# A transformer trunk on one core: gate and up by Strassen's scheme, with the first sum of weight blocks on GpSimd

## The chip, the core and the metric

The kernel runs on one core of a Trainium2 chip. The metric is the device time of one execution in microseconds (us). The kernel before takes 2266.12 us (median of 3 runs, 2264.7 to 2266.59).

## What is computed

The input is 512 rows of 1024 channels, and 16 learned rows are put in front of them, which makes 528 tokens. Four layers follow. Each is a mixer (pooling, differential attention, a conformer convolution, pooling again) and a SwiGLU feed-forward block, both added to the residual stream `h`; at the end there is an RMS norm. The change touches the feed-forward block alone:

```python
def swiglu_ffn(h, w_gate, w_up, w_down):
    return (jax.nn.silu(h @ w_gate) * (h @ w_up)) @ w_down
...
h = h + swiglu_ffn(rmsnorm(h, norm_ffn_g[i]), ffn_w_gate[i], ffn_w_up[i], ffn_w_down[i])
```

`w_gate` and `w_up` are 1024 x 2816 and `w_down` is 2816 x 1024, all float32. The last layer needs only the 512 real tokens.

## The kernel before

**Precision.** Every product of two float32 matrices is made of three products in the faster `fp32r` type. Each operand is split into a high part (a copy in `fp32r`, made by ScalarE) and a low part (the operand minus its high part, made by VectorE). TensorE then adds up hi x hi, hi x lo and lo x hi; `chunk` (L639) issues these three for one 128 x 128 block of weights. All data lies transposed: channels on the 128 partitions, tokens along the free axis. In layers 0 to 2 the 528 tokens are taken as two halves of 264, so a block of weights costs 6 matmuls of 264 columns. In layer 3 it costs 3 matmuls of 512 columns.

**The feed-forward block.** The 2816 hidden channels are 22 blocks of 128, called f. For each f, `pair_layer` (L714) makes gate and up: for either matrix 8 blocks of weights, one below the other, are summed in PSUM (the accumulator memory, 8 banks of 512 columns). That is 96 matmuls of 264 columns for one f, or 48 of 512. Banks 0 to 3 and 4 to 7 take turns. `out_layer` (L778) makes the down projection: for each of the 8 output blocks d, 22 blocks of weights, which is 132 matmuls.

**The weights.** A tile of weights (1024 columns, 512 KB) is loaded by SyncE's DMA queue into one of 4 slots of `w_raw`, copied to `w_hi` by ScalarE (`split_hi`, L1138), and subtracted into `w_lo` by VectorE (`split_lo`, L1354). TensorE waits for `lo_ready`, and a slot of `w_hi` is free again at `tile_used`.

**Order on the engines.** Each engine has its own program, written out by hand, and they meet by semaphores. `rounds` (L1152 for ScalarE, L1410 for VectorE) sets the order: the splits of the tiles two ahead, and then the epilogue of a block. The epilogue of an f (`pair`, L1527) is: VectorE scales gate and up out of PSUM by `rstd` (L1532, L1534), ScalarE takes the silu (L1192), VectorE multiplies (`hid`, L1538), ScalarE makes `hid_hi` (L1194) and VectorE `hid_lo` (L1540). The epilogue of a d adds the PSUM result to `h` (L1511) and makes the next layer's input `y_hi` (L1143) and `y_lo` (L1360). GpSimd squares the blocks of `h` and adds them up for the next norm (`sum_squares`, L532: L545 and L548). In the feed-forward block it does nothing else.

**Drain.** Where a VectorE instruction reads what the one before it wrote, the program puts a `drain` between them, as in the convolution (L1783).

Of the kernel before, what the change touches and what calls it, by code (L numbers as in the profile page):

```python
# [26 lines left out]
F32 = mybir.dt.float32  # L27
F32R = mybir.dt.float32r
I32 = mybir.dt.int32
ALU = mybir.AluOpType  # L30
# [24 lines left out]
LAM_INIT = 0.8 - 0.6 * math.exp(-0.3 * 1)  # L55
SLOT = 1024
SLOTS = 4
DOWN_SPLIT = (6, 6, 5, 5)
SPILL = 512 - HALF - META
MASKED = -1e30  # L60
LOWEST = -3e38
# [47 lines left out]
def plan():  # L109

    cols, first = [], {}

    def phase(name, sizes):
        first[name] = len(cols)
        cols.extend(sizes)
        assert len(cols) % SLOTS == 0

    for layer in range(4):
        if layer in (0, 3):
            phase(f"pool{layer}", [512] * 4)  # L120
# [6 lines left out]
        phase(f"up{layer}", [1024] * (2 * NF))  # L127
        phase(f"down{layer}", [n * P for n in DOWN_SPLIT] * NB)
    return cols, first


class Placer:
# [12 lines left out]
class Memory:  # L145


    def __init__(self, nc, ctx):
# [46 lines left out]
        self.pooled = new("pooled", [P, 2, TOK])  # L195

        new = Placer(nc, keep, end)
        self.hid_hi = new("hid_hi", [P, NF * TOK], F32R)
        self.hid_lo = new("hid_lo", [P, NF * TOK], F32R)
# [3 lines left out]
        self.hid = new("hid", [P, TOK])  # L203

        new = Placer(nc, keep, end)
        self.bias = new("bias", [P, HEADS * TOK])
# [61 lines left out]
class Semaphores:  # L268


    def __init__(self, sem):
# [72 lines left out]
        self.cv_lo_ready = sem("cv_lo_ready")  # L344
        self.out_turned = sem("out_turned")
        self.out_ready = sem("out_ready")


def wait(eng, sem, value):

    if not (isinstance(value, int) and value <= 0):
        eng.wait_ge(sem, value)
# [45 lines left out]
def trunk(nc, a, out):  # L398
# [3 lines left out]
    with ctx:  # L402
# [10 lines left out]
        def blk(t, d, t0=0, n=TOK):  # L413

            return t[:, ds(d * TOK + t0, n)]
# [5 lines left out]
        def banks(b, half):  # L421

            return ps[:, b, 0:SEQ] if half == SEQ else ps[:, b:b + 2, 0:half]

        block = ctx.enter_context(nc.Block())


        @block.sync
        def _(sp):
# [50 lines left out]
                             0, n * P)  # L480

            def load_ffn(layer):
                load_pairs(f"up{layer}", a["ffn_w_gate"][layer], a["ffn_w_up"][layer], NF)
                load_out(f"down{layer}", a["ffn_w_down"][layer], DOWN_SPLIT, 2)

            load_pool("pool0", 0)

# [30 lines left out]
        def _(pool):  # L518
# [13 lines left out]
            def sum_squares(r, hn):  # L532


                wait(pool, s.token_sums, r)
                wait(pool, s.rstd_sums, r)
                pool.memset(m.sumsq[:, :], 0.0)
# [32 lines left out]
            pool.drain().then_inc(s.rel_ready, 1)  # L570
            sum_windows(0)
            sum_squares(R_FFN0, H_POOL0)
            sum_squares(R_ATTN, H_FFN0)

            pool.wait_ge(s.tile_used, first["attn"])
# [37 lines left out]
                row_factors(hd - 1)  # L613
            row_factors(HEADS - 1)
            sum_squares(R_FFN1, H_ATTN)
            sum_squares(R_CONV, H_FFN1)
# [7 lines left out]
            sum_squares(R_FFN2, H_CONV)  # L624
            sum_squares(R_POOL3, H_FFN2)

            pool.wait_ge(s.tile_used, first["pool3"])
# [3 lines left out]
            pool.drain()  # L631
            sum_windows(1)
            sum_squares(R_FFN3, H_POOL3)
            sum_squares(R_FINAL, H_FFN3)


        @block.tensor
        def _(pe):
# [189 lines left out]
                        part(g, k)  # L828

            def ffn(layer, r, yn, hn, t0=0, half=HALF):  # L830
                e0 = NF * layer + (NB if layer >= 2 else 0)
                pair_layer(f"up{layer}", NF, e0, r, yn, hn, t0, half)
                out_layer(f"down{layer}", hn + 1, m.hid_hi, m.hid_lo, DOWN_SPLIT, 2, s.hidden_ready, NF * layer,
                          [(s.pairs_read, e0 + NF - 1), (s.pairs_read, e0 + NF)], t0, half)

            def project(h, par, c, k0, k1):

# [232 lines left out]
            attention_end()  # L1070
            ffn(1, R_FFN1, Y_FFN1, H_ATTN)

            pair_layer("conv_in", NB, 2 * NF, R_CONV, Y_CONV, H_FFN1, 0, HALF, conv=True)
            def fill(n):

                for _ in range(n):
# [52 lines left out]
        def _(act):  # L1129
            def split_hi(t, i, per, n):  # L1130

                if n == 0:
                    return
                slot = t % SLOTS
                act.wait_ge(raw_in[slot], (i * (per // SLOTS) + (t // SLOTS + 1)) * 16)
                if t >= SLOTS:
                    act.wait_ge(s.tile_used, i * per + (t - SLOTS + 1))
                act.activation(m.w_hi[:, slot, 0:n], m.w_raw[:, slot, 0:n], ACT.Copy).then_inc(s.hi_ready, 1)  # L1138
# [46 lines left out]
                        split_hi(tile0 + 4 + g, 0, 0, cols[tile0 + 4 + g])  # L1185

            def ffn(layer, hn, yn, row, t0=0, n=TOK):
                f0 = NF * layer

                def pair(f):  # L1190
                    act.wait_ge(s.gate_ready, f + (f0 + 1))
# [4 lines left out]
                rounds(f"up{layer}", NF, 2, NF // 2, pair)  # L1196
                rounds(f"down{layer}", NB, 4, NB // 2,
                       lambda d: None if row is None else y_hi(d, hn, yn, row, 0, TOK))

            def exponentials(h, j):  # L1200
# [103 lines left out]
            def conv_gate(c):  # L1304
                par = conv_parity[0] % 2
                conv_parity[0] += 1
                wait(act, s.conv_done, c - 1)
                for tap in range(TENSOR_TAPS):
                    for dst, w in ((m.tap_hi, m.vec_hi), (m.tap_lo, m.vec_lo)):
                        e = act.activation(dst[:, par, tap, :], m.ident[:, :], ACT.Copy,  # L1310
                                           scale=w[:, ds(c * ROWS + (ROW_DW + tap), 1)].bitcast(F32))
                e.then_inc(s.taps_ready, 1)
                act.wait_ge(s.pairs_read, c + (2 * NF + 1))
# [33 lines left out]
        def _(dve):  # L1347
# [173 lines left out]
                rounds(name, NB, per_group, n_rounds, low, None, early, add)  # L1521

            def ffn(layer, r, yn, row, t0=0, half=HALF):
                f0, e0, n = NF * layer, NF * layer + (NB if layer >= 2 else 0), SEQ if half == SEQ else 2 * half
                parity = [0]

                def pair(f):  # L1527
                    base = 4 * (parity[0] % 2)
                    parity[0] += 1
                    r2 = halves(m.rstd[:, t0:t0 + n], half)  # L1530
                    dve.wait_ge(s.tile_used, f * 2 + (first[f"up{layer}"] + 2))
                    dve.tensor_tensor(halves(m.gate[:, 0:n], half), banks(base, half), r2, ALU.mult)\  # L1532
                       .then_inc(s.gate_ready, 1)
                    dve.tensor_tensor(halves(m.up[:, 0:n], half), banks(base + 2, half), r2, ALU.mult)\  # L1534
                       .then_inc(s.pairs_read, 1)
                    dve.wait_ge(s.pairs_read, f + (e0 + 1))
                    dve.wait_ge(s.silu_ready, f + (f0 + 1))
                    dve.tensor_tensor(m.hid[:, 0:n], m.silu[:, 0:n], m.up[:, 0:n], ALU.mult).then_inc(s.hid_ready, 1)  # L1538
                    dve.wait_ge(s.hid_hi_ready, f + (f0 + 1))
# [323 lines left out]
```

## Time and profile before

| what | value |
|---|---|
| median of 3 runs | 2266.12 us |
| the profiled execution, its own time | 2268.74 us |
| its span, first to last instruction | 2267.0 us |
| mean granted TensorE clock (share of full speed) | 0.972 |
| busy: TensorE, its weight loads | 2146.5 us (95%), 2038.4 us (90%) |
| busy: VectorE, ScalarE, GpSimd | 1183.4 us (52%), 737.1 us (33%), 257.8 us (11%) |
| DMA | 180.9 MB, 80 GB/s |

The rows are one execution. A busy time is the time in which at least one instruction of an engine was running. TensorE's matmuls overlap, so their mean duration is longer than the distance from one start to the next, and it is that distance which counts. VectorE's instructions overlap a little as well (the next one starts before the last has written its end), so for them too the distance from start to start is the price.

### The profile page before, as it was taken

To read this page: it belongs to the slowest core of one execution; us is meant where nothing else is said; L and a number is where in the kernel's file an instruction comes from. 1 tells how busy PE (TensorE), PEld (TensorE's weight loads), DVE (VectorE), ACT (ScalarE), POOL (GpSimd) and SP (SyncE) were. 2 spreads that over 40 slices of the span, in tenths; PEclk is the share of its full clock that TensorE was granted. 3 is DMA by queue.
4 is the path that set the end of the run, shared out by engine and by line. 5 is a ranking of instruction groups with operands and counts; after the bars stand their busy time and mean duration, and the time that the engine had idled before them with its cause. 6 is when DMAs were issued, how large, how long until landed. Compare 5 with 4: busy or idle time off the path is not lost.

```text
span 2267.0 us, 40214 instructions
## 1 busy us (share of the span) xinstructions
PE 2146.5 (95%) x15690; PEld 2038.4 (90%) x15690; DVE 1183.4 (52%) x1900; ACT 737.1 (33%) x1222; POOL 257.8 (11%) x351
## 2 busy tenths in 40 slices
PE   5699999999998899999999999999999958999998
PEld 5699999999886899999999999999999956888886
DVE  6744443357776454444348996544444366444432
ACT  2333332234443233332236444322222222222220
POOL 4100001112122400000110000100001131000021
PEclk8899999999998899999999999999999989999999
DMA  3333323331111133332331111233323212333232
GB/s 101 107 90 92 93 77 94 90 113 50 53 56 47 47 89 90 89 93 77 91 99 51 41 52 36 85 86 93 93 76 91 84 56 83 93 93 93 84 94 73
DMA packets 339633, 180.90 MB, mean 80 GB/s; under 512 B 7068, under 2 KB 336797, under 8 KB 339558
## 3 DMA queue, kind: packets, MB, share of 16 engines
q1 hardware_dynamic: 337982, 175.01, 26.8%
q10 hardware_dynamic: 1048, 2.71, 0.3%
q0 software_dynamic: 528, 2.16, 0.3%
q8 instruction: 49, 0.80, 0.2%
q14 instruction: 26, 0.21, 0.0%
HBM read 177.74 MB, written 4.81 MB: 81 GB/s over the span
## 4 chain that ended last, share of the span: by engine, by line
PE 81%; DVE 8%; DVEq 5%; issue 4%; ACT 1%; POOLq 0%; DMA 0%; POOL 0%; SPq 0%; ACTq 0%
PE ps L644 76%; DVEq L1783 3%; DVE cv L1784 1%; DVE pool_s L1455 1%; PE ps L892 1%; PE ps L868 1%; PE ps L666 1%; DVE pooled L1466 1%; DVE w_lo L1354 1%; DVEq L1768 0%; DVE h L1476 0%; DVEq L1793 0%; PE ps L1077 0%; PE ps L674 0%; DMA meta_rows<-in_meta_tokens 0%
## 5 line engine op out<-in xcount | busy, mean ns | idle before, releaser
L644 PE MATMUL ps<-y_hi,w_hi 128*128 128x264 f32 (+1 forms) x3168 | 724.5, 301 | 67.3 <-DVE w_lo L1354 50.7
L644 PE MATMUL ps<-y_lo,w_hi 128*128 128x264 f32 (+1 forms) x3168 | 717.6, 299 | 0.0
L644 PE MATMUL ps<-y_hi,w_lo 128*128 128x264 f32 (+1 forms) x3168 | 715.4, 298 | 0.0
L644 PEld LDWEIGHTS ps<-y_hi,w_hi 128*128 128x128 f32 x3168 | 507.4, 190 | 92.6 <-issue 63.7
L644 PEld LDWEIGHTS ps<-y_lo,w_hi 128*128 128x128 f32 x3168 | 507.1, 190 | 15.3
L644 PEld LDWEIGHTS ps<-y_hi,w_lo 128*128 128x128 f32 x3168 | 506.0, 190 | 15.4
L1354 DVE TENSOR_TENSOR w_lo<-w_raw,w_hi 128x1024 fp32r<-128x1024 f32 (+3 forms) x376 | 426.9, 1168 | 157.6 <-ACT w_hi L1138 148.9
L1138 ACT ACTIVATE w_hi<-w_raw 128x1024 fp32r<-128x1024 f32 (+3 forms) x376 | 337.6, 930 | 221.1 <-PE ps L644 218.4
L644 PE MATMUL ps<-hid_hi,w_hi 128*128 128x264 f32 (+1 forms) x1232 | 283.8, 300 | 0.0
L644 PE MATMUL ps<-hid_hi,w_lo 128*128 128x264 f32 (+1 forms) x1232 | 283.6, 300 | 0.0
L644 PE MATMUL ps<-hid_lo,w_hi 128*128 128x264 f32 (+1 forms) x1232 | 283.4, 300 | 0.0
L1532 DVE TENSOR_TENSOR gate<-ps,rstd 128x528 f32<-128x528 f32 (+1 forms) x88 | 61.9, 704 | 406.2 <-PE ps L644 405.8
L1192 ACT ACTIVATE silu<-gate 128x528 f32<-128x528 f32 (+1 forms) x88 | 56.6, 643 | 618.6 <-DVE gate L1532 618.6
L545 POOL TENSOR_TENSOR square<-h 128x528 f32 x40 | 49.1, 1226 | 1400.5 <-DVE h L1511 1398.8
L644 PEld LDWEIGHTS ps<-hid_lo,w_hi 128*128 128x128 f32 x1232 | 197.1, 188 | 8.2
L644 PEld LDWEIGHTS ps<-hid_hi,w_lo 128*128 128x128 f32 x1232 | 196.7, 188 | 7.8
L644 PEld LDWEIGHTS ps<-hid_hi,w_hi 128*128 128x128 f32 x1232 | 195.9, 188 | 7.6
L1143 ACT ACTIVATE y_hi<-h,vec 128x528 fp32r<-128x528 f32 (+1 forms) x64 | 46.3, 733 | 298.8 <-DVE h L1511 199.4
L1511 DVE TENSOR_TENSOR h<-ps,h 128x528 f32 (+3 forms) x40 | 28.1, 703 | 191.1 <-PE ps L644 191.1
L1540 DVE TENSOR_TENSOR hid_lo<-hid,hid_hi 128x528 f32 (+3 forms) x88 | 62.0, 705 | 79.9 <-ACT hid_hi L1194 79.9
L1194 ACT ACTIVATE hid_hi<-hid 128x528 f32 (+3 forms) x88 | 56.5, 642 | 80.6 <-DVE hid L1538 80.6
L1360 DVE SCALAR_TENSOR_TENSOR y_lo<-h,vec,y_hi 128x528 fp32r<-128x528 f32 (+1 forms) x64 | 61.2, 976 | 29.2 <-ACT y_hi L1143 29.2
(228 smaller groups left out, 1982.3 us busy)
## 6 DMA issues: line engine op xcount, KB each, us to landing
w_raw<-in_ffn_w_gate SPq DMA_DIRECT2D x88, 512.0 KB, 3.9
w_raw<-in_ffn_w_up SPq DMA_DIRECT2D x88, 512.0 KB, 4.9
w_raw<-in_ffn_w_down SPq DMA_DIRECT2D x64, 384.0 KB, 3.5
w_raw<-in_ffn_w_down SPq DMA_DIRECT2D x64, 320.0 KB, 3.4
w_raw<-in_attn_w_qkv SPq DMA_DIRECT2D x16, 512.0 KB, 3.8
w_raw<-in_conv_w_in SPq DMA_DIRECT2D x16, 512.0 KB, 4.5
w_raw<-in_attn_w_qkv SPq DMA_DIRECT2D x16, 256.0 KB, 2.9
w_raw<-in_attn_w_o SPq DMA_DIRECT2D x8, 512.0 KB, 3.8
```

The source lines that it names most:

```text
L545: pool.tensor_tensor(m.square[:, :], blk(m.h, d), blk(m.h, d), ALU.mult)
L644: mm = pe.matmul(ps[:, bank + hf, 0:half], w[:, slot, col:col + P], x(hf), start=begin and w is m.w_hi and n == 0, stop=end and w is m.w_lo)
L1138: act.activation(m.w_hi[:, slot, 0:n], m.w_raw[:, slot, 0:n], ACT.Copy).then_inc(s.hi_ready, 1)
L1143: act.activation(blk(m.y_hi, d, t0, n), blk(m.h, d, t0, n), ACT.Copy, scale=vec_col(row, d))\
L1192: act.activation(m.silu[:, 0:n], m.gate[:, 0:n], ACT.Silu).then_inc(s.silu_ready, 1)
L1194: act.activation(blk(m.hid_hi, f, t0, n), m.hid[:, 0:n], ACT.Copy).then_inc(s.hid_hi_ready, 1)
L1354: dve.tensor_tensor(m.w_lo[:, slot, 0:n], m.w_raw[:, slot, 0:n], m.w_hi[:, slot, 0:n].bitcast(F32), ALU.subtract).then_inc(s.lo_ready, 1)
L1360: dve.scalar_tensor_tensor(out=blk(m.y_lo, d, t0, n), in0=blk(m.h, d, t0, n), scalar=vec_col(row, d), in1=blk(m.y_hi, d, t0, n).bitcast(F3 ...
L1511: e = dve.tensor_tensor(hd, banks(base, half), hd, ALU.add)
L1532: dve.tensor_tensor(halves(m.gate[:, 0:n], half), banks(base, half), r2, ALU.mult)\
L1540: dve.tensor_tensor(blk(m.hid_lo, f, t0, n), m.hid[:, 0:n], blk(m.hid_hi, f, t0, n).bitcast(F32), ALU.subtract).then_inc(s.hidden_ready, 1)
L1783: dve.drain()
```

## The change

**Blocks.** Four blocks f (the head) are made as before. The other 18 are taken as 9 pairs of f. For each pair and each of the two matrices the product is one of 2 x 2 blocks: the upper and lower 512 rows of the weights, the two blocks f, and the two halves of the tokens. Strassen's scheme (in the form with 7 products and shared sums) makes it of 7 products in place of 8. A product (`product` in `products`) is 4 blocks of weights x 3 = 12 matmuls of 264 columns (256 in layer 3), so a matrix of a pair is 84 matmuls, called a unit here.

**Factors from the tokens.** They are made once in a layer. VectorE writes the normed input out (`scaled_rows`, 8 instructions at f = 1), takes four differences (`factors_first`, `factors_second`) and makes the low parts `t_lo`; ScalarE makes the high parts `t_hi` (`factor_hi`).

**Factors from the weights.** They are made for each unit, in place in `w_raw`, in quarters of 512 columns. GpSimd adds quarter 1 to quarter 0 (`first_sums`). VectorE makes the other three sums in two instructions of 512 and 1024 columns (`other_sums`). The 7 factors are split in three steps of 1536, 1024 and 1024 columns (`operands_hi` on ScalarE, `operands_lo` on VectorE). The factors of gate lie in `w_hi` and `w_lo`, those of up in `y_hi` and `y_lo`, which nothing else needs at that time.

**Results.** The 7 products of a unit fill 7 banks. ScalarE copies the first out (`snaps`). VectorE adds the rest up (`add_c11`, `add_c22`, `add_c21`: 528, 528 + 264 and 528 columns). For a pair there is one silu of 1056 columns, one multiplication (`mix`), one `mixed_hi` and one `mixed_lo`.

**Down.** The projection is made in parts: one of 4 hidden blocks after the head, one after each two pairs (three of them, in a loop), and a last one of 6 hidden blocks at the end. Every part but the last is added to `h` by VectorE (`add_part`, 4 instructions of 1056 columns).

**The order on VectorE and TensorE**, which the prediction follows:

```diff
+                def operands_lo(i, q, kind, step):
...
+                    c0, c1, sub = ((1, 4, 0), (2, 4, 3), (0, 2, 5))[step - 1]
+                    hi, lo = ring[kind]
+                    at = slice(sub * SUB, (sub + c1 - c0) * SUB)
+                    dve.wait_ge(s.op_hi, i * 12 + (3 * mat + step))
+                    dve.tensor_tensor(lo[:, at], raw_of(kind, c0, c1), hi[:, at].bitcast(F32), ALU.subtract)\
+                       .then_inc(s.op_lo, 1)
+                def other_sums(i, q, kind):
+                    dve.drain()
+                    dve.wait_ge(s.first_sums, i * 4 + (matrix_of(layer, q, kind) + 1))
+                    dve.tensor_tensor(raw_of(kind, 2, 3), raw_of(kind, 0, 1), raw_of(kind, 2, 3), ALU.subtract)
+                    dve.drain()
...
+                    dve.tensor_tensor(two, two, s2, ALU.subtract).then_inc(s.sums_ready, 1)
+                def prepare(i, q, kind):
+                    operands_lo(i, q, kind, 1)
+                    other_sums(i, q, kind)
+                def product_pair(i, q, b, begin, second, third):
+                    if b:
+                        mix(i, q - 1)
+                    prepare(i, q, "up")
+                    add_c11(i, q, "gate")
+                    if b:
+                        mixed_lo(i, q - 1, b - 2)
+                    operands_lo(i, q, "up", 2)
+                    add_c22(i, q, "gate")
+                    operands_lo(i, q, "up", 3)
+                    add_c21(i, q, "gate")
+                    begin()
+                    add_c11(i, q, "up")
+                    second()
+                    add_c22(i, q, "up")
+                    third()
+                def part(i, j):
+                    if j > 0:
+                        mix(i, 2 * j - 1)
+                        mixed_lo(i, 2 * j - 1, 2)
+                    add_part(i, j, 0)
+                    add_part(i, j, 1)
+                    prepare(i, 2 * j, "gate")
+                    add_part(i, j, 2)
+                    operands_lo(i, 2 * j, "gate", 2)
+                    add_part(i, j, 3)
+                    operands_lo(i, 2 * j, "gate", 3)
...
+                rounds(f"up{layer}", HEAD_F, 2, HEAD_F // 2, pair, lambda: rstd_of(r, RMS_EPS))
+                factors_second()
+                for c in (2, 3):
+                    split_lo(part0 + c, 0, 0, SLOT)
+                factor_lo(3, T3, 2, x_blocks(True, hw))
+                factor_lo(4, T4, 2, x_blocks(False, hw))
+                part(0, 0)
+                with dve.Fori(0, MID_PARTS) as i:
+                    product_pair(i, 0, 0, *next_gate(i, 1))
+                    product_pair(i, 1, 2, lambda: [tile_lo(i, 1, c) for c in (0, 1)],
+                                 lambda: tile_lo(i, 1, 2), lambda: tile_lo(i, 1, 3))
+                    part(i, 1)
```

Here `begin`, `second` and `third` of most pairs are the three steps of the next pair's gate (`next_gate`); before a part they are the low parts of its four tiles (`tile_lo`). TensorE's unit, with the products numbered as they are issued:

```diff
+                    pe.wait_ge(s.op_lo, i * 12 + (3 * mat + 1))
...
+                    product(1, B11, int(kind == "up"))
+                    if not fresh:
+                        pe.wait_ge(s.c11_ready, i * 4 + mat)
+                    product(2, B21, 2)
+                    pe.wait_ge(s.op_lo, i * 12 + (3 * mat + 2))
+                    product(3, T2, 3)
+                    pe.wait_ge(s.op_lo, i * 12 + (3 * mat + 3))
...
+                        pe.wait_ge(s.c22_ready, i * 4 + mat)
+                    product(5, T1, 5)
+                    product(6, T3, 4)
+                    if not fresh:
+                        pe.wait_ge(s.c21_ready, i * 4 + mat)
+                    product(4, B22, 7)
+                    product(0, T4, 6)
```

and GpSimd's new work, put between the sums of squares of two norms:

```diff
+            def first_sums(layer):
+                def one(i, q):
+                    for kind, slot in (("gate", 0), ("up", 2)):
+                        pool.wait_ge(raw_in[slot], i * 48 + raw_count(layer, q))
+                        pool.tensor_tensor(raw_of(kind, 0, 1), raw_of(kind, 0, 1), raw_of(kind, 1, 2), ALU.add)\
+                            .then_inc(s.first_sums, 1)
```

## Rows read from the trace of the kernel before

**Rows 1.** The page, part 1: busy us (share of the span) x instructions.

```profile
PE 2146.5 (95%) x15690; PEld 2038.4 (90%) x15690; DVE 1183.4 (52%) x1900; ACT 737.1 (33%) x1222; POOL 257.8 (11%) x351
```

**Rows 2.** The chain that ended last: start us, us, what.

```profile
98.13 375.36 PE ps L644 x3072
...
805.45 375.12 PE ps L644 x3072
...
1459.09 369.50 PE ps L644 x3024
...
1899.72 351.09 PE ps L644 x1512
```

**Rows 3.** Busy time by stretch; columns in the first line.

```profile
core 0: us, PE busy (x) PEld busy (x) DVE busy (x) ACT busy (x) POOL busy (x), PEclk, DMA share, GB/s
98.13:473.49 375.36, 375.36 (x3075) 375.36 (x3075) 158.41 (x179) 122.94 (x146) 23.47 (x19) 1.00 0.31 89
...
1899.72:2250.81 351.09, 351.08 (x1512) 283.85 (x1512) 143.91 (x167) 90.68 (x116) 22.41 (x14) 1.00 0.30 87
```

**Rows 4.** Timeline of VectorE, layer 0, one f: start, us, what, idle before.

```profile
139.53 0.71 DVE L1532 TENSOR_TENSOR gate<-ps,rstd 128x528 f32<-128x528 f32 x1 [4.00 <-PE ps L644]
140.16 0.70 DVE L1534 TENSOR_TENSOR up<-ps,rstd 128x528 f32<-128x528 f32 x1
141.03 0.71 DVE L1538 TENSOR_TENSOR hid<-silu,up 128x528 f32<-128x528 f32 x1 [0.17 <-ACT silu L1192]
142.66 0.71 DVE L1540 TENSOR_TENSOR hid_lo<-hid,hid_hi 128x528 f32 x1 [0.93 <-ACT hid_hi L1194]
143.49 2.36 DVE L1354 TENSOR_TENSOR w_lo<-w_raw,w_hi 128x1024 fp32r<-128x1024 f32 x2
151.28 0.71 DVE L1532 TENSOR_TENSOR gate<-ps,rstd 128x528 f32<-128x528 f32 x1 [5.43 <-PE ps L644]
```

**Rows 5.** Timeline of VectorE, convolution's output projection.

```profile
1409.98 1.23 DVE L1354 TENSOR_TENSOR w_lo<-w_raw,w_hi 128x1024 fp32r<-128x1024 f32 x1 [0.38 <-ACT w_hi L1138]
1411.12 0.76 DVE L1360 SCALAR_TENSOR_TENSOR y_lo<-h,vec,y_hi 128x528 fp32r<-128x528 f32 x1
1411.80 0.77 DVE L1513 SCALAR_TENSOR_TENSOR h<-ps,vec,h 128x528 f32<-128x528 f32 x1
```

**Rows 6.** Timeline of VectorE, convolution; a drain stands before each cv.

```profile
1309.01 0.76 DVE L1784 SCALAR_TENSOR_TENSOR cv_odd<-cv_u,vec,cv_odd 128x528 f32<-128x528 f32 x1
1309.94 0.77 DVE L1784 SCALAR_TENSOR_TENSOR cv<-cv_u,vec,cv 128x528 f32 x1 [0.17 <-issue]
1310.63 0.76 DVE L1784 SCALAR_TENSOR_TENSOR cv_odd<-cv_u,vec,cv_odd 128x528 f32<-128x528 f32 x1
...
1313.81 1.88 DVE L1784 SCALAR_TENSOR_TENSOR cv<-cv_u,vec,cv 128x528 f32 x1 [0.18 <-issue]
1315.61 0.76 DVE L1784 SCALAR_TENSOR_TENSOR cv_odd<-cv_u,vec,cv_odd 128x528 f32<-128x528 f32 x1
```

**Rows 7.** Timeline of GpSimd in the same stretch.

```profile
1313.80 1.32 POOL L622 TENSOR_TENSOR cv_sum<-cv_sum,cv 128x528 f32<-128x528 f32 x1 [20.81 <-DVE cv L1756]
```

**Rows 8.** Groups of GpSimd: x count | busy us, mean ns | idle before.

```profile
L548 POOL TENSOR_TENSOR sumsq<-sumsq,square 128x528 f32<-128x528 f32 x40 | 67.0, 1675 | 5.8 <-issue 0.3
```

**Rows 9.** Timeline of ScalarE, layer 0.

```profile
152.02 0.65 ACT L1192 ACTIVATE silu<-gate 128x528 f32<-128x528 f32 x1 [7.62 <-DVE gate L1532]
...
154.27 1.28 ACT L1138 ACT_TABLE_LOAD   x1
155.56 2.01 ACT L1138 ACTIVATE w_hi<-w_raw 128x1024 fp32r<-128x1024 f32 x2
```

**Rows 10.** The page, part 6: DMA issues, KB each, us to landing.

```profile
w_raw<-in_ffn_w_gate SPq DMA_DIRECT2D x88, 512.0 KB, 3.9
w_raw<-in_ffn_w_up SPq DMA_DIRECT2D x88, 512.0 KB, 4.9
```

**Rows 11.** Busy time by stretch, columns as in rows 3: pooling, layer 3.

```profile
1830.00:1900.00 70.00, 38.52 (x197) 32.93 (x198) 56.81 (x90) 14.74 (x23) 26.88 (x22) 0.78 0.16 46
```

More of the change, by code:

```diff
@@ L57 @@
 SLOTS = 4
-DOWN_SPLIT = (6, 6, 5, 5)
+HEAD_F = 4
+MID_PARTS = 3
+LAST_PAIRS = 3
+FFN_PAIRS = 2 * MID_PARTS + LAST_PAIRS
+LAST_F = 2 * LAST_PAIRS
+PRODUCTS = 7
+SUB = SLOT // 2
+(B11, B21, B22, T3, T1, T4, T2) = range(PRODUCTS)
 SPILL = 512 - HALF - META
@@ L126, in plan, with pairs_done @@
             phase("conv_out", [1024] * NB)
-        phase(f"up{layer}", [1024] * (2 * NF))
-        phase(f"down{layer}", [n * P for n in DOWN_SPLIT] * NB)
+        phase(f"up{layer}", [1024] * (2 * HEAD_F))
+        phase(f"part{layer}", [1024] * (4 * (1 + MID_PARTS)))
+        phase(f"down{layer}", [LAST_F * P] * NB)
     return cols, first
+def pairs_done(first, t):
+    return FFN_PAIRS * sum(t >= first[f"down{layer}"] for layer in range(4))
 class Placer:
@@ L830, in ffn @@
             def ffn(layer, r, yn, hn, t0=0, half=HALF):
[L831 to L834, printed above, removed]
+                e0 = HEAD_F * layer + (NB if layer >= 2 else 0)
+                hw = min(half, SEQ // 2) if half == SEQ else half
@@ new lines, in ffn, with bank_of, products, product @@
+                part0, down0 = first[f"part{layer}"], first[f"down{layer}"]
+                parts0 = 4 * (1 + MID_PARTS) * layer
+                def bank_of(d):
+                    return (0, 1, 4, 5)[d % 4] if half == SEQ else 2 * (d % 4)
+                def products(i, q, kind):
+                    mat = matrix_of(layer, q, kind)
+                    fresh = kind == "gate" and q in (0, 2 * MID_PARTS)
+                    hi, lo = ring[kind]
+                    read = parts0 + 2 * q
+                    def product(sub, t, bank):
+                        for k in range(4):
+                            at = sub * SUB + k * P
+                            for n, (w, b) in enumerate(((hi, m.t_hi), (hi, m.t_lo), (lo, m.t_hi))):
+                                mm = pe.matmul(ps[:, bank, 0:hw], w[:, at:at + P], b[:, t, k, 0:hw],
+                                               start=k == 0 and n == 0, stop=k == 3 and n == 2)
+                        mm.then_inc(s.products, 1)
+                    pe.wait_ge(s.op_lo, i * 12 + (3 * mat + 1))
+                    if fresh:
+                        pe.wait_ge(s.part_read, i * 4 + (read + 3))
+                    elif q not in (0, 2 * MID_PARTS):
+                        pe.wait_ge(s.snaps, i * 4 + (mat - 1))
+                    product(1, B11, int(kind == "up"))
[5 more added lines that the diff above has]
+                    pe.wait_ge(s.op_lo, i * 12 + (3 * mat + 3))
+                    if fresh:
+                        pe.wait_ge(s.part_read, i * 4 + (read + 4))
+                    else:
+                        pe.wait_ge(s.c22_ready, i * 4 + mat)
[5 more added lines that the diff above has]
+                    product(0, T4, 6)
@@ new lines, in ffn @@
+                pair_layer(f"up{layer}", HEAD_F, e0, r, yn, hn, t0, half)
+                part(0, 0)
+                pe.wait_ge(s.t_ready, 4 * (layer + 1))
+                with pe.Fori(0, MID_PARTS) as i:
+                    for q in range(2):
+                        products(i, q, "gate")
+                        products(i, q, "up")
+                    part(i, 1)
+                for q in range(2 * MID_PARTS, FFN_PAIRS):
+                    products(0, q, "gate")
+                    products(0, q, "up")
@@ L836, in project @@
+                down()
             def project(h, par, c, k0, k1):
@@ L1198, in ffn, with down_tiles @@
+                def down_tiles():
+                    act.wait_ge(s.products, PRODUCTS * (2 * pair_of(layer, FFN_PAIRS) - 1))
+                    for c in range(2):
+                        split_hi(down0 + c, 0, 0, LAST_F * P)
+                product_pair(0, FFN_PAIRS - 1, 2 * LAST_PAIRS - 2, down_tiles, nothing, nothing)
+                mixed_hi(0, FFN_PAIRS - 1, 2 * LAST_PAIRS - 2)
+                rounds(f"down{layer}", NB, 1, 2,
                        lambda d: None if row is None else y_hi(d, hn, yn, row, 0, TOK))
@@ new lines, in add_c22 @@
+                def add_c22(i, q, kind):
+                    dst = m.gate4 if kind == "gate" else m.up4
+                    mat = matrix_of(layer, q, kind)
+                    dve.wait_ge(s.c11_ready, i * 4 + (mat + 1))
+                    dve.wait_ge(s.products, i * 28 + (PRODUCTS * mat + 5))
+                    g = dst[:, 1:2, 0:hw].to_broadcast([P, 2, hw])
+                    dve.tensor_tensor(two, ps[:, 4:6, 0:hw], g, ALU.add)
+                    dve.drain()
+                    dve.tensor_tensor(dst[:, 3, 0:hw], ps[:, 5, 0:hw], two[:, 0], ALU.add).then_inc(s.c22_ready, 1)
@@ new lines, in add_c21, with mix @@
+                def add_c21(i, q, kind):
+                    dst = m.gate4 if kind == "gate" else m.up4
+                    dve.wait_ge(s.products, i * 28 + PRODUCTS * (matrix_of(layer, q, kind) + 1))
+                    dve.tensor_tensor(dst[:, 1:3, 0:hw], ps[:, 6:8, 0:hw], two, ALU.add).then_inc(s.c21_ready, 1)
+                def mix(i, q):
+                    pr = pair_of(layer, q)
+                    add_c21(i, q, "up")
+                    dve.wait_ge(s.silu_parts, i * 2 + (pr + 1))
+                    dve.wait_ge(s.c21_ready, i * 4 + (2 * pr + 2))
+                    dve.tensor_tensor(m.up4[:, :, 0:hw], m.up4[:, :, 0:hw], m.gate4[:, :, 0:hw], ALU.mult)                       .then_inc(s.hid_mixed, 1)
@@ new lines, in ffn @@
+                for n_pair in range(LAST_PAIRS - 1):
+                    q = 2 * MID_PARTS + n_pair
+                    product_pair(0, q, 2 * n_pair, *next_gate(0, q + 1))
+                product_pair(0, FFN_PAIRS - 1, 2 * LAST_PAIRS - 2,
+                             lambda: [split_lo(down0 + c, 0, 0, LAST_F * P) for c in range(2)], nothing, nothing)
+                mix(0, FFN_PAIRS - 1)
+                mixed_lo(0, FFN_PAIRS - 1, 2 * LAST_PAIRS - 2)
+                out_rounds(f"down{layer}", 1, 2, half, t0, None, yn, row, (0, 2, 4, 6))
```

310 lines of the change are left out of this document (297 added, 13 removed).

## The prediction, made before the changed kernel was run

> **What bounds the kernel now.** I read the busy shares first: TensorE 95%, VectorE 52%, ScalarE 33%, GpSimd 11% [rows 1]. The chain that ended last then shows where that is without a gap: in the feed-forward block of each layer it is one unbroken run of TensorE, 375 us with 3072 matmuls in layers 0 and 1, 369.5 with 3024 in layer 2, 351 with 1512 in layer 3 [rows 2]. The stretches say the same from the other side: TensorE is busy for all of the 375.36 us at clock 1.00, VectorE for 158, ScalarE for 123, GpSimd for 23 [rows 3]. So here every matmul less is worth its distance to the next, as long as nothing else becomes late. A matmul of 264 columns costs 375.36 / 3072 = 0.1222 us, one of 512 costs 351.09 / 1512 = 0.2322.
>
> **What is removed.** A unit is 84 matmuls where there were 96, and there are 18 units in a layer: 216 less. The down projection keeps its 1056. Layers 0 to 2: 3 x 216 x 0.1222 = 79.2 us. In layer 3 the units have matmuls of 256 columns in place of 512, which the trace doesn't show. Half of 0.2322 is 0.1161; the price of 264 columns, 0.1222, is the other end; the straight line through the two known prices gives 0.1186, and I take that, since 264 is so near. Before: 18 x 48 x 0.2322 = 200.6 us; after: 1512 x 0.1186 = 179.3; saved 21.3 (15.9 to 25.1). In all 100.5 us (95 to 104). A unit now lasts 84 x 0.1222 = 10.3 us, a pair 20.5, where it was 23.5.
>
> **VectorE's prices.** From start to start 528 columns take 0.63 us (139.53 to 140.16) [rows 4], 1024 take 1.14 (1409.98 to 1411.12) [rows 5]. That is 1.03 ns a column and 0.09 us besides: 264 cost 0.36, 512 cost 0.61, 1056 cost 1.17, 1536 cost 1.67, 2112 cost 2.26. A drain makes 0.93 of 0.69: 0.24 us [rows 6].
>
> **VectorE in a unit.** Splits 1.67 + 1.14 + 1.14, sums 0.61 + 1.14, additions 3 x 0.63 + 0.36, three drains 0.72: 8.7 us. `mix` and `mixed_lo` add 2.34 to a pair: 19.7 against TensorE's 20.5. Alone, VectorE would just keep up.
>
> **The sum on GpSimd.** It takes 0.61 us off VectorE per unit. But one GpSimd addition of 528 columns started at 1313.80 and took 1.32 us [rows 7], and the VectorE instruction that started 0.01 later took until 1315.61 for its successor to start, 1.80 in place of 0.69 [rows 6]. So two instructions with two SBUF inputs each do not run side by side, and VectorE loses 1.1 us. (GpSimd waits in its turn: its mean is 1.68, not 1.32 [rows 8].) PSUM additions are too few to count on; nearly every sum will meet a split. Net, the move costs VectorE up to 0.5 us per unit in place of saving 0.6. With it a pair takes VectorE 19.7 + 2.2 = 21.9 us.
>
> The Trainium skill speaks against this edit (GPSIMD Engine Reference, Engine selection and Key points): it keeps two-input elementwise work on VectorE, calls GpSimd some two times slower at it, and says that the two share SBUF interfaces when VectorE has two SBUF inputs. The trace agrees on both, 1.32 against 0.63 us and 1.80 against 0.69. By the rule the deficit per pair is on the path; that is the second rival.
>
> **Why I still leave TensorE the bound.** A late VectorE does not stop TensorE at once. Factors are made one unit ahead: by my order of the instructions the third split of a unit is done some 11 to 12 us after the unit before it began, and the product that needs it starts at 10.3 + 3 x 1.47 = 14.7. That is a reserve of about 3 us, the deficit is 1.4 per pair with a mix, and after two pairs comes a part with 192 matmuls (23.5 us) in which VectorE has 4 x 1.17 for `add_part`, `mix`, `mixed_lo` and one matrix to prepare: some 15 us. Over pairs and middle parts of a layer TensorE has 9 x 20.5 + 3 x 23.5 = 255 us, VectorE about 9 x 21.9 + 3 x (4.7 + 4.6) = 225.
>
> **What is added on the path.** (a) Entry into the products. From the end of f = 3 VectorE has: its epilogue until 3.8 (139.53 to 142.66 and 0.63 more) [rows 4], three differences with two drains 4.0, two tiles 2.3, two low parts 2 x 2.26, one or two meetings with GpSimd, first `add_part` 1.17: done at 15.8 to 18. TensorE has only 96 matmuls, 11.7 us, until it needs the banks that this addition frees. Stall 5 us (4 to 6.3). The rest of VectorE's extra work in the head is covered: at f = 1 eight instructions of 0.69 push the tile for f = 3 to 10.5 us after the end of f = 1, and it is needed at 11.7; if I am 1.2 us out there, that comes on top. (b) Each middle part. After the last product come `add_c21` 0.63, `mix` 1.41, ScalarE's copy 1.1, `mixed_lo` 1.3: 4.5 us, under 48 matmuls that don't need it, 5.9 us. But VectorE comes 2 to 3 late from the pair with a mix, and the tiles of the part land 4 to 5 us after the up factors are split [rows 10]. I take 1.2 us (0 to 3), three times. (c) The same at the last part: 1 us (0 to 3). Per layer 5 + 3.6 + 1 = 9.6, in all 38 us (16 to 73).
>
> **Costed at nothing.** ScalarE has in a unit 3584 columns of copies (1024 take 1.0 [rows 9]), a copy of 264 and half of two instructions of 1056: about 5 of 10.3 us; a table load of 1.28 at a loop's turn fits in. DMA moves the same bytes; a unit's two tiles have a whole pair to land. SyncE's waits stand in the order in which the slots come free. GpSimd has 2 x 1.7 of 20.5 us; the memset that now waits for `h` (0.5) is behind a block of 36 matmuls, 4.4 us, of which its two sums take 3. In the last part VectorE has per block 0.63 + 0.69 + 0.88 and one or two meetings: under 4.4.
>
> **The sum.** 100.5 - 38.4 = 62 us less. The profiled execution took 2268.7 us, so 2206.6; the median of the runs is 2.6 lower: 2204. With the ends of all terms 95 - 73 = 22 and 104 - 16 = 88: 2178 to 2244.
>
> **Rivals.**
> 1. *No stalls to speak of.* The reserves hold everywhere and the entry costs 2 us or less: 100 less 8, 2174 or below. For it: VectorE is idle in more than half of the stretch now. Against: the entry's list of VectorE work is long, whichever way I order it. 0.10.
> 2. *VectorE becomes the bound in the pairs.* Every pair takes its 21.9 us, 1.4 over TensorE, 36 times: 50 us, and the entry's 20: 100 - 70 = 30 less, 2236. For it: a meeting costs more than the sum itself. Against: the parts give the reserve back. 0.20.
> 3. *Slower: ScalarE and VectorE take turns and neither runs ahead.* In a unit the second split can't start before VectorE's sums and ScalarE's copy of them, the first not before a copy of 1536 which needs the ring free. If both copies are waited for, 1.5 and 1.3 us, a unit takes 8.7 + 1.2 + 1.1 + 2.8 = 13.8 us, a pair 27.5 against 23.5 before: 36 x 4 + 20 = 164 us more, 2430. With the other stalls as I have them it decides from 10.3 + 62 / 72 = 11.1 us a unit on. For it: `hid_lo` waits 0.93 us for ScalarE now [rows 4], so such hops are not free. Against: ScalarE is half idle, and between the steps VectorE has additions to do. 0.11.
> 4. *The clock.* In a stretch where TensorE idles 31 of 70 us the granted clock is 0.78, in the full ones 1.00 [rows 3, 11]. If each entry stall drew a time as long at half speed behind it, that would be 10 to 20 us more: inside my range, not a case of its own. That the products cost another price than 0.1222 (other weights for each matmul, where now two share one): 0.03, about 2240.
>
> **Chances.** My case 0.56. With what can be told from no change being 0.2% (4.5 us): faster 0.86, same 0.03, slower 0.11. The range of 2172 to 2246 leaves out rival 3, the far side of 1 and the top of 2.
>
> **What would show it.** In layers 0 to 2 216 matmuls fewer each, and units of 10.3 us at clock 1.00; in layer 3 units of 10.0. VectorE waiting for TensorE's products in most units, not TensorE for `op_lo`. VectorE splits of 1536 near 1.7 us, some of them 1.1 longer beside `first_sums`. TensorE's longest wait in each layer on `add_part`, about 5 us, four times. It is wrong if TensorE waits for `w_lo` or for the additions in every unit, if a unit is over 11 us, or if the entry takes over 8.

## The result and the profile after

The changed kernel takes 2189.98 us (median of 4 runs, 2188.9 to 2191.29), the kernel before, beside it, 2265.41 (4 runs). The ratio is 0.9667, with a 95% interval of 0.965 to 0.9684: 75 us less. I had forecast 2204, 62 less. The profiled execution's span is 2188.8 us, where it was 2267.0.

First the page's part 1, to be held against [rows 1]:

```profile
PE 2054.2 (94%) x15690; PEld 1983.2 (91%) x15690; DVE 1647.5 (75%) x2284; ACT 824.9 (38%) x1240; POOL 381.2 (17%) x423
```

TensorE is busy for 92 us less, and VectorE for 464 more: it has gone from half to three quarters of the time. The number of matmuls is the same by chance: 648 fewer in layers 0 to 2, 648 more in layer 3, where matmuls of 512 columns became nearly twice as many of 256.

The chain that ended last, layer 0 and a piece of layer 3 (start us, us, what). Where [rows 2] had one run of 375 us, there are now these:

```profile
95.98 29.62 PE ps L776 x240
...
134.01 2.27 DVE w_lo L1706 x2
136.28 4.54 DVE t_lo L1894 x2
142.14 14.50 PE ps L776 x96
156.64 40.79 PE ps L982 x336
197.43 23.34 PE ps L776 x192
220.77 40.79 PE ps L982 x336
261.55 23.34 PE ps L776 x192
...
349.02 61.19 PE ps L982 x504
410.21 40.88 PE ps L776 x336
...
1893.54 39.78 PE ps L982 x336
...
2079.81 59.68 PE ps L982 x504
```

L982 is the new `product`, four units in 40.79 us. From 156.64 on each piece begins where the last one ended: in the pairs and in the middle parts TensorE waits for nothing. The chain leaves TensorE at one place, the entry, between the head and the first unit, where it goes through VectorE's list.

What TensorE waited for in the whole execution (us in total, times, longest); of the list this is the one wait in the feed-forward blocks that the kernel before did not have:

```profile
PE ps L776 <- DVE h L2036: 18.7, 4, 4.9
```

L2036 is `add_part`. Four waits, one in each layer. And the stretches of the chain above, with the granted clock (the column behind the POOL one):

```profile
core 0: us, PE busy (x) PEld busy (x) DVE busy (x) ACT busy (x) POOL busy (x), PEclk, DMA share, GB/s
137.00:142.10 5.10, 0.26 (x3) 0.05 (x1) 5.10 (x4) 2.25 (x2) 2.84 (x1) 0.90 0.63 187
142.10:156.60 14.50, 14.46 (x98) 14.49 (x99) 7.03 (x6) 1.06 (x1) 0.00 (x0) 0.80 0.00 1
156.60:197.40 40.80, 40.80 (x339) 40.80 (x338) 36.35 (x38) 19.91 (x21) 4.47 (x3) 1.00 0.48 138
197.40:220.80 23.40, 23.40 (x195) 23.40 (x194) 12.23 (x10) 3.64 (x3) 1.94 (x2) 1.00 0.12 32
```

Behind the wait TensorE's clock is 0.80 of full speed on average, part of the time at its lower level, and 96 matmuls take 14.5 us. In the products the clock is 1.00, and VectorE is busy for 36 of 41 us (89%); in the middle part, the last of these stretches, it is busy for 12 of 23 (52%).

**The account.** Products, layers 0 to 2: 3 x 40.79 + 61.19 = 183.6 us for 18 units, before 18 x 96 x 0.1222 = 211.2 [rows 2]: 27.6 less, three times. Layer 3: 3 x 39.78 + 59.68 = 179.0, before 200.6: 21.6 less. In all 104.4. Against it stand the waits, 18.7 us, and the matmuls behind them: 14.50, 13.44, 13.46 and 14.09 us in the four layers, where 96 matmuls cost 11.7 and the 48 long ones of layer 3 cost 11.1, together 9.3 us more than that. 104.4 - 18.7 - 9.3 = 76 us; measured 75 between the medians, 78 between the spans of the two profiled executions.

### The profile page after: what moved, and what is told of

It is laid out like the page before. It is cut to its first block, busy times and chain, and to the rows that moved or that the text cites. A ratio compares the mean times of both kernels' runs of the same rounds, so it can differ in the third digit from the quotient of the medians.

```text
span 2188.8 us, 40039 instructions
## 1 busy us (share of the span) xinstructions
PE 2054.2 (94%) x15690; PEld 1983.2 (91%) x15690; DVE 1647.5 (75%) x2284; ACT 824.9 (38%) x1240; POOL 381.2 (17%) x423
## 4 chain that ended last, share of the span: by engine, by line
PE 77%; DVE 10%; DVEq 5%; issue 4%; POOLq 1%; ACT 1%; DMA 0%; POOL 0%; SPq 0%; ACTq 0%
PE ps L776 39%; PE ps L982 33%; DVEq L2312 3%; DVE cv L2313 1%; DVE pool_s L1807 1%; DVE w_lo L1706 1%; PE ps L1117 1%; PE ps L1141 1%; DVE t_lo L1894 1%; PE ps L798 1%; POOLq L663 1%; DVE pooled L1818 1%; POOLq L660 0%; DVEq L2297 0%; DVE h L1828 0%
## 5 line engine op out<-in xcount | busy, mean ns | idle before, releaser
L776 PE MATMUL ps<-y_hi,w_hi 128*128 128x264 f32 (+1 forms) x1152 | 260.3, 303 | 66.3 <-DVE w_lo L1706 50.7
L776 PE MATMUL ps<-hid_hi,w_hi 128*128 128x264 f32 (+1 forms) x1232 | 288.1, 303 | 18.7 <-DVE h L2036 18.7
L982 PE MATMUL ps<-t_lo,y_hi 128*128 128x264 f32 (+1 forms) x1008 | 285.9, 284 | 0.0
L982 PE MATMUL ps<-t_lo,w_hi 128*128 128x264 f32 (+1 forms) x1008 | 285.9, 284 | 0.0
L982 PE MATMUL ps<-t_hi,y_lo 128*128 128x264 f32 (+1 forms) x1008 | 285.3, 283 | 0.0
L982 PE MATMUL ps<-t_hi,w_lo 128*128 128x264 f32 (+1 forms) x1008 | 285.3, 283 | 0.0
L982 PE MATMUL ps<-t_hi,y_hi 128*128 128x264 f32 (+1 forms) x1008 | 284.9, 283 | 0.0
L982 PE MATMUL ps<-t_hi,w_hi 128*128 128x264 f32 (+1 forms) x1008 | 284.8, 283 | 0.0
L776 PEld LDWEIGHTS ps<-y_hi,w_hi 128*128 128x128 f32 x1152 | 185.3, 193 | 78.1 <-issue 62.5
L776 PE MATMUL ps<-y_lo,w_hi 128*128 128x264 f32 (+1 forms) x1152 | 251.5, 296 | 0.0
L776 PE MATMUL ps<-y_hi,w_lo 128*128 128x264 f32 (+1 forms) x1152 | 251.1, 295 | 0.0
L776 PEld LDWEIGHTS ps<-hid_hi,w_hi 128*128 128x128 f32 x1232 | 199.5, 192 | 27.6 <-issue 19.7
L982 PEld LDWEIGHTS ps<-t_hi,w_hi 128*128 128x128 f32 x1008 | 189.7, 188 | 0.2
L982 PEld LDWEIGHTS ps<-t_hi,y_hi 128*128 128x128 f32 x1008 | 189.7, 188 | 0.0
L982 PEld LDWEIGHTS ps<-t_lo,w_hi 128*128 128x128 f32 x1008 | 189.4, 188 | 0.2
```

The lines of the kernel that those rows point to most:

```text
L776: mm = pe.matmul(ps[:, bank + hf, 0:half], w[:, slot, col:col + P], x(hf), start=begin and w is m.w_hi and n == 0, stop=end and w is m.w_lo)
L982: mm = pe.matmul(ps[:, bank, 0:hw], w[:, at:at + P], b[:, t, k, 0:hw], start=k == 0 and n == 0, stop=k == 3 and n == 2)
```

## The experiments

Times are medians of 4 executions, the ratios are to the kernel before on the same chip; "changed" is the changed kernel, 2190.

### The first sum back on VectorE

```diff
                 def other_sums(i, q, kind):
-                    dve.drain()
-                    dve.wait_ge(s.first_sums, i * 4 + (matrix_of(layer, q, kind) + 1))
+                    dve.tensor_tensor(raw_of(kind, 0, 1), raw_of(kind, 0, 1), raw_of(kind, 1, 2), ALU.add)
+                    dve.drain()
```

with the four calls of `first_sums` on GpSimd taken out.

> The first sum is made by VectorE, as one more addition of 512 columns in front of the other sums; GpSimd does nothing in the products. Theory A (TensorE bounds the pairs; the sum is hidden wherever it is made): two pairs keep their 81.6 us (4 units of 20.4), and only the entry gains a little, since no GpSimd addition meets VectorE there: 2 to 6 us less than the changed kernel's 2190, 2184 to 2188. Rival B (taking the sum off VectorE is what lets it keep up): 72 units with 0.61 us more, up to 44 us slower, 2234. Rival C (the meetings with GpSimd do cost on the path): 72 x 0.5 = 36 us faster, 2154.

Measured: 2186.93 us, ratio 0.9649 (0.9633 to 0.9665). That is 3 us under the changed kernel, and the two intervals overlap, so the times alone don't tell the two apart. The trace says where a difference is. Its chain has the same 40.79, 23.34 and 61.19 us pieces, so in the pairs the place of the sum changes nothing. The waits at the entry are 16.0 us in place of 18.7:

```profile
PE ps L772 <- DVE h L2032: 16.0, 4, 4.1
```

Theory A holds. Half of the change's name, the sum on GpSimd, brings nothing here; by the waits it costs about 3 us, at the entry, where GpSimd's addition holds one VectorE instruction up. In the changed kernel VectorE's `hid` in the last epilogue of the head took 1.61 us with GpSimd's addition beside it; here the same instruction takes 0.71. Changed kernel, VectorE and then GpSimd (start us, us, instruction):

```profile
127.12 1.61 DVE L1926 TENSOR_TENSOR hid<-silu,up 128x528 f32<-128x528 f32 x1 [0.17 <-ACT silu L1449]
```

```profile
126.88 1.28 POOL L685 TENSOR_TENSOR w_raw<-w_raw 128x512 f32<-128x512 f32 x1 [42.43 <-DMA w_raw<-in_ffn_w_gate]
```

### The order at the entry

```diff
+                    if j == 0:
+                        factor_lo(3, T3, 2, x_blocks(True, hw))
+                        factor_lo(4, T4, 2, x_blocks(False, hw))
                     prepare(i, 2 * j, "gate")
...
                     split_lo(part0 + c, 0, 0, SLOT)
-                factor_lo(3, T3, 2, x_blocks(True, hw))
-                factor_lo(4, T4, 2, x_blocks(False, hw))
                 part(0, 0)
```

The new lines stand in VectorE's `part`, behind the first two `add_part`.

> As the changed kernel, but at the entry VectorE makes the last two low parts of the token factors after the first two add_part and not before them. Theory A: the four waits of TensorE for add_part (18.7 us in all) go, and with them the matmuls at a lower clock behind them (14.5, 13.4, 13.5 and 14.1 us where 96 of 264 cost 11.7 and 48 of 512 cost 11.1: 9 us in all): 28 us less, 2162. Rival B: the low parts come too late and TensorE waits for them in place of the addition: 2185 to 2195. Rival C: the lower clock has another cause than the wait: 19 us less, 2171.

Measured: 2162.94 us, ratio 0.9544 (0.9528 to 0.956), 27 us under the changed kernel. Theory A, with both of its terms. The waits for `add_part` have shrunk from 18.7 to 0.6 us, and the 96 matmuls in front of the first unit run at full clock (columns as above):

```profile
138.08:150.00 11.92, 11.92 (x98) 11.92 (x99) 11.73 (x8) 2.72 (x3) 3.17 (x1) 1.00 0.21 62
821.71:833.62 11.91, 11.91 (x97) 11.91 (x98) 11.71 (x8) 2.71 (x3) 3.06 (x1) 1.00 0.22 64
```

The low parts that were moved are needed only by the first unit, 11.9 us later. TensorE's wait had been for the bank that `add_part` frees, behind 4.5 us of work that nobody was waiting for. With the next one this is the fastest of all the versions.

### Both together

The edits of the two before it.

> The reordered entry of e2 with the first sum on VectorE as in e1. What e1 gained (3 us) came from the entry, where GpSimd no longer held VectorE up; with the entry's waits gone there is nothing left of it. Theory A: the same as e2, 2163, within 2 us. Rival: the two gains add up, 2160 or less; or VectorE, with 0.61 us more per unit and the low parts made later, comes late in the first unit: 2166 to 2175.

Measured: 2163.55 us, ratio 0.9547 (0.9531 to 0.9563), the same as with the new order alone. With the entry's wait gone the place of the sum shows nowhere.

### One product less: the sum on GpSimd

```diff
-                        for k in range(4):
+                        for k in range(1 if sub == 0 else 4):
...
-                            for n, (w, b) in enumerate(((hi, m.t_hi), (hi, m.t_lo), (lo, m.t_hi))):
+                            for n, (w, b) in enumerate(((hi, m.t_hi), (hi, m.t_lo), (lo, m.t_hi))[:1 if sub == 0 else 3]):
```

> Leaves out work: the last product of each unit is one matmul in place of 12 (its result isn't the reference's). The sum stays on GpSimd. Theory A (TensorE alone bounds a unit, and VectorE, at 10 to 11 us a unit with its meetings, becomes the bound below that): 792 matmuls at 0.12 would be 95 us less, but only 45 to 75 come, 2115 to 2145, and TensorE waits for VectorE in the pairs. Rival B (VectorE has far more reserve): all 95, 2095. Rival C (the unit is bound by a chain and not by TensorE already now): under 20 us less.

Measured: 2168.41 us, 22 under the changed kernel, of the 95 that the matmuls are worth. Between theory A (45 and more) and rival C (under 20): the reserve is smaller than I, and theory A, had it. What TensorE waits for now:

```profile
PE ps L776 <- DVE hid_lo L1996: 33.8, 12, 3.9
PE ps L776 <- DVE h L2036: 18.9, 4, 4.8
PE ps L982 <- DVE y_lo L1940: 12.5, 27, 0.6
```

`hid_lo` is the low part before each middle part, `y_lo` the splits. So 22 us came, 0.3 us a unit, and 73 didn't. The new waits are 46 of these, and 34 of the 46 stand before the twelve middle parts. Some 10 more are the clock: six of the nine middle parts of layers 0 to 2 ran partly at the lower level behind that wait, 144 matmuls in 19.2 to 20.3 us in place of 17.8. Two of them (columns as above):

```profile
201.59:220.91 19.32, 19.32 (x146) 19.32 (x147) 8.59 (x7) 2.55 (x2) 0.00 (x0) 0.91 0.01 1
329.59:347.40 17.81, 17.81 (x146) 17.81 (x147) 8.59 (x7) 2.56 (x2) 0.00 (x0) 1.00 0.00 0
```

The 0.3 us is therefore what the whole kernel gained per unit and not the reserve of a unit. The chain into the wait is not VectorE's alone either. Before each of the twelve middle parts it passes through the landing of a tile for the down projection, 3.4 to 5.3 us after its issue, which VectorE's last split has released; ScalarE's copy, `mix`, `mixed_hi` and `mixed_lo` follow:

```profile
188.51 5.31 DMA w_raw<-in_ffn_w_down
193.84 1.07 ACT w_hi L1483
199.58 1.96 DVE hid_lo L1996
```

### One product less: the sum on VectorE

The same, with the sum of the first experiment.

> Leaves out the same work as the run before it, but VectorE makes the first sum. With VectorE the bound, the place of the sum must show. Theory A (a meeting costs VectorE 1.1 us, the sum 0.61): 10 to 36 us faster than with the sum on GpSimd. Rival B (meetings cost VectorE less than the sum): 10 to 44 us slower than with the sum on GpSimd.

Measured: 2179.23 us, 11 slower than with the sum on GpSimd; the intervals, 0.9602 to 0.9634 here and 0.9557 to 0.9602 there, just touch. Rival B, and against my theory A: where VectorE is late, the sum on GpSimd helps, by 0.15 us per unit. TensorE's waits agree: for `y_lo` 22.3 us in place of 12.5. So a meeting of the two costs less than the 0.61 us that the sum costs.

### More work for VectorE

```diff
+                    if step > 1:
+                        dve.tensor_tensor((m.y_lo if step == 2 else m.y_hi)[:, 7 * SUB:8 * SUB], raw_of(kind, c0, c0 + 1),
+                                          hi[:, sub * SUB:(sub + 1) * SUB].bitcast(F32), ALU.subtract)
```

> As the changed kernel, and VectorE makes two more subtractions of 512 columns per unit, whose results nobody reads (1.22 us a unit, the output is the same). With one twelfth to one seventh of TensorE's work taken out, only 0.3 us a unit came off, so VectorE's reserve is small. Theory A (reserve of about 0.3 us a unit, VectorE the bound from there): 72 x (1.22 - 0.3) = 66 us slower than the changed kernel, 2256, within 20. Rival B (my prediction: the middle parts give the reserve back, since VectorE is busy 146 of 192 us there): under 20 us slower, 2195 to 2210.

Measured: 2244.64 us (2238.68 to 2249.38), ratio 0.9902 (0.9881 to 0.9924): 55 us slower than the changed kernel. That is 0.76 us a unit of the 1.22 that were added, so some 0.46 were free. Theory A within its bounds, and rival B, which is the step of my prediction on the middle parts, falls: they give back too little. TensorE waits at the same places as with a product less:

```profile
PE ps L982 <- DVE y_lo L1943: 20.4, 26, 1.2
PE ps L776 <- DVE h L2039: 18.3, 4, 4.7
PE ps L776 <- DVE hid_lo L1999: 18.3, 12, 2.5
```

In one stretch of twelve units (156 to 356) VectorE is now busy for 160 of 200 us and is nevertheless what TensorE waits for. Of the other 40 us it waits 27 in the middle parts, for TensorE's products that `add_part` reads. In the pairs themselves (157.0 to 204.6) it is busy for 42.9 of 47.6 us, 90%, and most of the rest are drains and short waits for ScalarE's copies. So the mean of the stretch, 80%, hides that it is nearly full where it is waited for.

### GpSimd made to meet VectorE

```diff
                         pool.wait_ge(raw_in[slot], i * 48 + raw_count(layer, q))
+                        pool.wait_ge(s.op_hi, i * 12 + (3 * matrix_of(layer, q, kind) + 1))
```

> As the changed kernel, but GpSimd's addition also waits for the first high part of its unit, so that it starts together with VectorE's split of 1536 columns (two SBUF inputs). Theory A (two such instructions don't run side by side; in the changed kernel they mostly miss each other because the landing of the tile, which releases the addition, falls where VectorE reads PSUM or waits): the split of 1536, or the sum behind it, comes 1.1 to 1.3 us later in every unit, VectorE is the bound, 40 to 75 us slower, 2230 to 2265. Rival B (meetings are cheap in themselves, about 0.2 us): the split stays under 2.0 us, and 0 to 15 us slower.

Measured: 2186.95 us, ratio 0.9648 (0.9632 to 0.9664). Theory A is wrong on the time: no loss at all, and the waits at the entry are the 16.0 us of the first experiment. Rival B comes nearer on the time, but some splits took over its 2.0 us. That the two don't run side by side is right. VectorE's timeline:

```profile
158.14 1.76 DVE L1941 TENSOR_TENSOR y_lo<-w_raw,y_hi 128x1536 fp32r<-128x1536 f32 x1
161.09 0.69 DVE L1948 TENSOR_TENSOR w_raw<-w_raw 128x512 f32<-128x512 f32 x1 [1.18 <-POOL w_raw L686]
...
168.22 2.23 DVE L1941 TENSOR_TENSOR w_lo<-w_raw,w_hi 128x1536 fp32r<-128x1536 f32 x1
...
177.95 2.08 DVE L1992 TENSOR_TENSOR up<-up,gate 128x1056 f32<-128x1056 f32 x1
```

and GpSimd's:

```profile
158.19 2.86 POOL L686 TENSOR_TENSOR w_raw<-w_raw 128x512 f32<-128x512 f32 x1 [16.18 <-ACT y_hi L1478]
167.43 1.41 POOL L686 TENSOR_TENSOR w_raw<-w_raw 128x512 f32<-128x512 f32 x1 [6.38 <-ACT w_hi L1478]
177.63 1.29 POOL L686 TENSOR_TENSOR w_raw<-w_raw 128x512 f32<-128x512 f32 x1 [8.79 <-ACT y_hi L1478]
```

The one that starts first goes through at its own pace and the other waits until about its end. At 158.14 VectorE was first by 0.05 us: it took its 1.76, GpSimd took 2.86 in place of 1.28, and VectorE then stood 1.18 us for the sum. At 168.22 and 177.95 GpSimd had been running, and VectorE's instructions took 2.23 in place of 1.75 and 2.08 in place of 1.26. Over the whole run VectorE waited 33.1 us for these sums, and its splits of 1536 columns and `mix` took some 23 us more, while others took some 14 less than in the changed kernel. The balance, by the groups of the two traces, is about 0.6 us a unit more than in the changed kernel, and it cost no time; the run before this one had 0.46 free. Why a little more than that went by without a loss isn't shown.

## Why the prediction was right, step by step

- **TensorE bounds the pairs: right.** Units of 10.2 us at clock 1.00, no wait in the products in any layer. I had 10.3.
- **What is removed: right, a little low.** 104.4 us against 100.5. A product's matmul of 264 columns cost 40.79 / 336 = 0.1214, not 0.1222. The unknown price of 256 columns was 39.78 / 336 = 0.1184, where the line through two known prices gave 0.1186.
- **VectorE in a unit: right.** From start to start its instructions cost 1.14 us for 1024 columns (166.74 to 167.88) and 0.34 for 264 (166.40 to 166.74), where I had 1.14 and 0.36. Two units in a row started 9.3 us apart (159.15 and 168.49), of which 0.5 was waiting and 0.3 a meeting with GpSimd; I had 8.7 without either. VectorE's timeline, then GpSimd's:

```profile
159.15 1.76 DVE L1940 TENSOR_TENSOR y_lo<-w_raw,y_hi 128x1536 fp32r<-128x1536 f32 x1
...
162.99 0.70 DVE L1966 TENSOR_TENSOR gate<-ps,sumsq 128x528 f32<-128x528 f32 x1
164.20 1.50 DVE L1940 TENSOR_TENSOR y_lo<-w_raw,y_hi 128x1024 fp32r<-128x1024 f32 x1 [0.51 <-ACT y_hi L1477]
...
166.40 0.43 DVE L1977 TENSOR_TENSOR gate<-ps,square 128x264 f32<-128x264 f32 x1
166.74 1.22 DVE L1940 TENSOR_TENSOR y_lo<-w_raw,y_hi 128x1024 fp32r<-128x1024 f32 x1
167.88 0.70 DVE L1983 TENSOR_TENSOR gate<-ps,square 128x528 f32<-128x528 f32 x1
168.49 1.75 DVE L1940 TENSOR_TENSOR w_lo<-w_raw,w_hi 128x1536 fp32r<-128x1536 f32 x1
...
200.69 1.68 DVE L1996 TENSOR_TENSOR hid_lo<-up,hid_hi 128x1056 fp32r<-128x1056 f32 x1 [1.16 <-ACT hid_hi L1503]
```

```profile
163.32 1.30 POOL L685 TENSOR_TENSOR w_raw<-w_raw 128x512 f32<-128x512 f32 x1 [21.38 <-DMA w_raw<-in_ffn_w_gate]
172.04 1.52 POOL L685 TENSOR_TENSOR w_raw<-w_raw 128x512 f32<-128x512 f32 x1 [7.42 <-DMA w_raw<-in_ffn_w_up]
```

- **(a) The entry: right in the mechanism.** Waits of 4.7 us on average where I had 5, on the instruction I named: in layer 0 VectorE was done with it at 142.0, 16.4 us after the end of f = 3 (125.60), where I had 15.8 to 18. The clock behind them, 9 us in all, I had mentioned as 10 to 20 and left out of the sum. The new order shows both: 27 us.
- **(b) and (c), the parts: wrong.** I took 1.2 us three times and 1 once a layer, 18 us in all; measured nothing. The chain from the last product to `mixed_lo` was 4.5 to 4.9 us in two middle parts that I read, under 5.9 of other matmuls, as worked out. I had added a delay for a VectorE that comes late from the pair with a mix, because each meeting stood in my list with 1.1 us.
- **The price of a meeting: wrong in size, and with it the net of the change's second half.** I took the one clean case of the old trace [rows 6, 7], 1.1 us, for the price of every sum. The groups of the changed kernel say otherwise (x count, busy us, mean ns):

```profile
L1940 DVE TENSOR_TENSOR y_lo<-w_raw,y_hi 128x1024 fp32r<-128x1024 f32 x72 | 92.1, 1280 | 8.2 <-ACT y_hi L1477 8.2
L1951 DVE TENSOR_TENSOR w_raw<-w_raw 128x1024 f32<-128x1024 f32 x72 | 92.0, 1278 | 5.3
L1940 DVE TENSOR_TENSOR y_lo<-w_raw,y_hi 128x1536 fp32r<-128x1536 f32 x36 | 63.2, 1755 | 1.4
```

  Against the kernel with the sum on VectorE, where the first two have 1218 and 1225 ns and the third 1754, the splits, sums and low parts (those of the down projection's tiles and of `hid` included) lost some 13 us in 72 meetings: 0.2 us each. None of the splits of 1536 columns was held up, though I had expected some of them to take 1.1 us longer. In a typical round one of the two additions begins while VectorE adds from PSUM or waits for ScalarE: 163.32 falls behind a PSUM addition (162.99) and costs the next split 0.28 us; 172.04 costs nothing. The addition is released by the landing of a tile (875 + 221 us of GpSimd's waiting is for that), and the load by VectorE's own third split, so it falls at the same place of VectorE's list each time, and that place is mild. That it is this timing was tried from one side: moved onto the splits, the additions cost 0.6 us more a unit, 0.8 in place of 0.2.
- **The reserve: right for the splits, too large before the parts.** The third split of the unit shown above is done at 167.96, 11.3 us after the unit before it began (156.64), and the product that needs it starts at about 171.2: the 3 us that I had. But `mixed_lo` before the first middle part is done at 202.37, and TensorE needs it 48 matmuls behind 197.43, at 203.3: 0.9 us, for four units together. What a pair is late shows there first. I had said that the parts give the reserve back; with more work for VectorE 0.46 us of 1.22 a unit were free, and the rest cost time. The forecast didn't fail on it because the meetings were cheap, and that is luck. By an estimate from that run, meetings of 1.1 us in place of 0.2 would have cost 72 x (0.9 - 0.46) = 32 us: some 2222, a little nearer to the second rival (2236) than to my 2204.
- **The rules of the Trainium skill** (GPSIMD Engine Reference, Engine selection and Key points). Their first half, keep two-input elementwise work on VectorE, the runs bear out here only at the entry, by waits of 3 us; with a product less, where VectorE is late, it would have been the wrong choice, by 11 us. Their second half, the shared interfaces, shows wherever the sum is on GpSimd: 1.61 us for `hid` in place of 0.71.

Of the signs that I gave, units of 10.2 us at clock 1.00 and the wait of about 5 us for `add_part`, four times, came. Two didn't: the longer splits of 1536, and VectorE waiting for TensorE's products in most units; it waited for them in some 15 of the 72, all of them up units (15 waits in `add_c11`, 12 in `add_c22`, 12 in `add_c21`), those before the middle parts among them.

The two errors, waits that weren't there (+18) and a clock loss left out (-9), together with 4 us on the matmuls and 1 at the entry make the 14 us between 2204 and 2190. That the two errors went opposite ways is luck too: had the clock cost nothing, the forecast would have been 23 us off.

What stays open: whether a still earlier load of the down projection's tiles, with more slots, would raise the reserve. Their landing is in the chain before every middle part once a product is left out, which speaks for it, but it wasn't tried.

## What to carry to other kernels

When an engine at 95% is relieved, list what its waits will hang on at each seam between two kinds of work, and order the other engine's list there by who waits for what: moving two instructions behind two others was worth 27 us, a third of what all of Strassen's scheme brought. A second engine busy 76% of the time can have next to no reserve: here the 76% were 89% in the pairs and 52% in the parts. Look at each kind of stretch by itself, and find out by adding work to it or taking some from the first. Two engines that exclude each other cost what the phase between them makes of it: one clean collision in the old trace cost 1.1 us, the mean of 72 meetings 0.2.

## What the runs showed that I had not expected

- The exclusion of VectorE and GpSimd goes to the one that started first: with VectorE ahead by 0.05 us (158.14) it was GpSimd that took 1.6 us longer; in the old trace, with GpSimd ahead by 0.01 us, it was VectorE, by 1.1 [rows 6, 7].
- Four waits of TensorE of under 5 us each cost half as much again behind them: in layers 0 to 2 96 matmuls took 13.4 to 14.5 us in place of 11.9, at a mean clock of 0.80 to 0.87.
- GpSimd's sums of squares are nearly the bound of the last part now. The chain in layer 2 runs through them, 3.9 us a block (squares 1.4, sum 1.9, gaps), against TensorE's 4.4. TensorE's wait for their end is 4.1 us, where it was 3.9, so they cost nothing more yet:

```profile
1741.62 1.39 POOLq L660
1743.12 1.91 POOLq L663
1745.55 1.39 POOLq L660
```
